# Sums of squares of the delta rule: an exact split into three bf16 numbers on GpSimd instead of one f32 product

## The reference

```python
def l2norm(x):
    xf = x.astype(jnp.float32)
    return (xf * lax.rsqrt(jnp.sum(xf * xf, axis=-1, keepdims=True) + 1e-6)).astype(x.dtype)
...
        q = l2norm(qkv[..., :GDN_KEY_DIM].reshape(bn, length, GDN_QK_HEADS, GDN_HEAD_DIM)) * (GDN_HEAD_DIM ** -0.5)
        k = l2norm(qkv[..., GDN_KEY_DIM:2 * GDN_KEY_DIM].reshape(bn, length, GDN_QK_HEADS, GDN_HEAD_DIM))
...
    def finish(o, z):
        bn_, _, length, _ = o.shape
        o = rmsnorm(o.transpose(0, 2, 1, 3), g_norm).reshape(bn_, length, GDN_VAL_DIM)
        return (o.astype(z.dtype) * jax.nn.silu(z)) @ w_out
```

## Time and profile before

| | |
|---|---|
| median of three runs | 3255.62 us |
| lowest and highest | 3249.88 and 5628.62 us |
| span of the profiled execution, first to last instruction | 3251.1 us |
| TensorE products busy | 3092.5 us, 95% |
| VectorE busy | 1731.2 us, 53% |
| ScalarE busy | 1539.1 us, 47% |
| GpSimd busy | 873.2 us, 27% |
| mean granted TensorE clock, share of full speed | 0.978 |

### The profile page before, as it was taken

One profiled execution on the slowest core, in us unless ns is written; L12 is line 12 of the kernel. 1 busy time (PEld: TensorE's weight loads), 2 busy tenths in 40 slices (PEclk: granted clock), 3 DMA queues, 4 the chain that ended last, 5 costly groups with the idle time before them and its releaser, 6 DMA issues. The chain is left out here.

```text
span 3251.1 us, 55663 instructions
## 1 busy us (share of the span) xinstructions
PE 3092.5 (95%) x21673; PEld 2016.4 (62%) x21673; DVE 1731.2 (53%) x3543; ACT 1539.1 (47%) x3296; POOL 873.2 (27%) x652
## 2 busy tenths in 40 slices
PE   5889999999999999999999999897999999999998
PEld 3357777777777764455445555444777777777753
DVE  1156666666666652244443334346676767776632
ACT  3155555555555531256432444335655565555521
POOL 0044434533533410011001101003544435343400
PEclk9699999999999999999999999898999999999999
DMA  9921111211211126022311111102212222121135
GB/s 375 330 68 54 56 56 55 67 56 45 72 56 51 45 89 235 1 68 64 128 33 31 29 46 52 72 4 80 66 53 69 59 60 63 57 68 53 43 120 192
DMA packets 224097, 261.93 MB, mean 81 GB/s; under 512 B 19418, under 2 KB 158948, under 8 KB 223716
## 3 DMA queue, kind: packets, MB, share of 16 engines
q1 hardware_dynamic: 223844, 258.46, 24.7%
HBM read 239.15 MB, written 19.27 MB: 79 GB/s over the span
## 5 line engine op out<-in xcount | busy, mean ns | idle before, releaser
L898 PE MATMUL ps<-hT,W 128*128 128x512 f32 (+1 forms) x2656 | 1001.2, 506 | 3.0 <-DVEq L192 2.0
L898 PEld LDWEIGHTS ps<-hT,W 128*128 128x128 f32 x2656 | 470.5, 193 | 195.1 <-issue 165.6
L1331 DVE CAST_PREDICATED arena<-mask,ps 128x384 bf16<-128x384 uint32 x448 | 253.2, 565 | 223.2 <-PE ps L967 174.3
L1148 ACT CAST arena<-ps 128x384 bf16<-128x384 f32 x384 | 166.9, 482 | 347.7 <-PE ps L954 346.7
L2372 PE MATMUL ps<-arena 128*128 128x512 f32 x712 | 311.2, 595 | 2.3 <-SPq L192 2.0
L1333 DVE CAST_PREDICATED arena<-mask,ps 128x384 bf16<-128x384 uint32 x448 | 250.9, 560 | 0.0
L2372 PEld LDWEIGHTS ps<-arena 128*128 128x128 f32 x712 | 134.5, 191 | 167.1 <-issue 162.8
L2007 PE MATMUL ps<-hT,W 128*128 128x512 f32 (+1 forms) x608 | 218.2, 493 | 0.6 <-DMA W<-in_att_w_in 0.4
L1455 POOL TENSOR_TENSOR arena<-arena 128x768 f32<-128x768 f32 (+1 forms) x32 | 44.4, 1389 | 636.0 <-ACT arena L1192 636.0
L1268 DVE SCALAR_TENSOR_TENSOR arena<-arena,vec 128x770 f32<-128x770 f32 (+1 forms) x192 | 205.4, 1070 | 6.8
L967 PEld LDWEIGHTS ps<-arena 128*128 128x128 bf16 x2304 | 144.7, 98 | 55.4 <-issue 51.0
(11 more groups left out here) (284 smaller groups left out, 6177.0 us busy)
## 6 DMA issues: line engine op xcount, KB each, us to landing
arena<-in_ada_w SPq DMA_DIRECT2D x24, 2048.0 KB, 19.5
W<-in_gdn_w_in SPq DMA_DIRECT2D x95, 512.0 KB, 4.0
arena<-decay_sums SPq DMA_DIRECT2D x64, 384.0 KB, 4.1
W<-decay_rows SPq DMA_DIRECT2D x64, 384.0 KB, 5.0
arena<-in_gdn_w_out SPq DMA_DIRECT2D x32, 512.0 KB, 10.5
W<-in_gdn_w_out SPq DMA_DIRECT2D x30, 512.0 KB, 3.4
arena<-gated SPq DMA_DIRECT2D x32, 384.0 KB, 7.7
gated<-arena SPq DMA_DIRECT2D x24, 384.0 KB, 2.3
```

The lines of the kernel that those rows point to most:

```text
L898: mm = pe.matmul(ps[:, b, 0:t1 - t0], w[:, i, :], env.hT[:, i, t0:t1], start=(i == 0), stop=(i == KD - 1))
L1148: act.copy(half_cols(Xb[d], s, d), ps[:, 2 * d, 0:384].rearrange("p (c b s) -> p c b s", c=NT, s=s)).then_inc(*inxe.up(m, lv, d))
L1331: dve.copy_predicated(half_cols(Mb[d], s, d), wide(env.m4[:, d, lv]), src_m).then_inc(*inm.up(m, lv, d, "m"))
```

## The change

One f32 square on GpSimd becomes five instructions: the square, its cast to bf16 (high part), the difference to it, the cast of the difference (middle part), and the difference to that, written as bf16 (low part). Each waits for the one before by a semaphore. The three parts add up to the f32 square. TensorE sums them by three bf16 products with a bf16 matrix of ones in one PSUM group, where one f32 product with f32 ones was. The matrix of ones is cast once per layer. The same holds for tiles (`squares`) and outputs.

```diff
-                    ("vtok", (NT, P)), ("ktok", (NT, P)), ("sz", (2, T)), ...
+                    ("vtok", (NT, P)), ("ktok", (NT, P)), ("sqhib", (T,)), ("sqmidb", (T,)), ("sqlowb", (T,)), ("onesb", (P,)), ("sz", (2, T)), ...
...
+    sqp = seq("x_parts", [(n, i) for n in TILES for i in range(4)])
+    osp = seq("o_parts", [(m, i) for m in U for i in range(4)])
...
-                mm = pe.matmul(ps[:, b, 0:t1 - t0], env.ones, v.sq[:, t0:t1], start=True, stop=True)
+                for part_at, exact in enumerate((v.sqhib, v.sqmidb, v.sqlowb)):
+                    mm = pe.matmul(ps[:, b, 0:t1 - t0], v.onesb, exact[:, t0:t1], start=(part_at == 0), stop=(part_at == 2))
...
+        def split(t, lo, parts, done, n):
+
+            whole, hi, mid, low = v.sq[:, lo:T], v.sqhib[:, lo:T], v.sqmidb[:, lo:T], v.sqlowb[:, lo:T]
+            pool.tensor_tensor(whole, t[:, lo:T], t[:, lo:T], ALU.mult).then_inc(*parts.up(n, 0))
+            pool.wait_ge(parts.sem, parts.at(n, 0))
+            pool.tensor_copy(hi, whole).then_inc(*parts.up(n, 1))
+            pool.wait_ge(parts.sem, parts.at(n, 1))
+            pool.tensor_tensor(whole, whole, hi, ALU.subtract).then_inc(*parts.up(n, 2))
+            pool.wait_ge(parts.sem, parts.at(n, 2))
+            pool.tensor_copy(mid, whole).then_inc(*parts.up(n, 3))
+            pool.wait_ge(parts.sem, parts.at(n, 3))
+            pool.tensor_tensor(low, whole, mid, ALU.subtract).then_inc(*done.up(n))
...
-            pool.tensor_tensor(v.sq[:, lo:T], t[:, lo:T], t[:, lo:T], ALU.mult).then_inc(*sqx.up(n))
-
+            split(t, lo, sqp, sqx, n)
+
+        pool.tensor_copy(v.onesb, env.ones)
...
-                ot = v.OT[:, n % 2, LO:T]
-                pool.tensor_tensor(v.sq[:, LO:T], ot, ot, ALU.mult).then_inc(*osq.up(n))
+                split(v.OT[:, n % 2], LO, osp, osq, n)
```

More of the change, by code:

```diff
@@ L635, in gdn_phase @@
     v = carve(env, [("pad", (2, PADW)), ("acc", (2, CONVW)), ("q", (T,)), ("k", (T,)), ("kS", (T,)), ("sq", (T,)),
-                    ("vtok", (NT, P)), ("ktok", (NT, P)), ("sz", (2, T)), ("KK", (NT, P)), ("QK", (NT, P)),
+                    ("vtok", (NT, P)), ("ktok", (NT, P)), ("sqhib", (T,)), ("sqmidb", (T,)), ("sqlowb", (T,)), ("onesb", (P,)), ("sz", (2, T)), ("KK", (NT, P)), ("QK", (NT, P)),
                     ("OT", (2, T)), ("S", (2, P)), ("R", (2, P)), ("V", (2, P)), ("VK", (2, P)), ("offneg", (P,)),
```

## The result

| | before | after |
|---|---|---|
| median of the runs | 3252.75 us (4 runs) | 3330.57 us (4 runs) |
| ratio, 95% interval | | 1.0251 [1.0228, 1.0275] |
| span of the profiled execution | 3251.1 us | 3333.8 us |
| TensorE products busy | 3092.5 us | 3102.0 us |
| mean granted clock | 0.978 | 0.971 |

A forecast was written before the change was run, and what follows sets the result against it. TensorE, busy throughout its slots, was taken as the bound. Losses of 65.6 us less a gain of 16.2 made net +49 us; 3251.1 + 49.4 + 4.5 = 3305 us, 1.5% slower, range 3258 to 3345.

The forecast's parts named there:

- TensorE's gain, 16.2: Sums in both delta layers: three bf16 products save 0.19 us per large sum, 0.10 per small, 16.2 us in all.
- rival 4: Sums: bf16 products of 512 columns stream at twice the packed rate, a large sum saves 0.52 us; 3284 us; 3%.
- Exposed waits, 21: Output sums in slots 14 and 15 of both layers: TensorE waits for the split, 21 us lost.
- The turns on the ports: Boundary after an even unit: VectorE and GpSimd alternate on shared SBUF ports; in layer 0 L1331 starts 3.6 us late.
- Rival 1: VectorE keeps the ports over back-to-back pairs, so only the exposed waits count: +5, 3260 us; 22%.
- Boundary in layer 0, 17.5: Seven boundaries after even units in layer 0: 2.5 us of TensorE stall each at L1012, 17.5 us.
- Odd slots in layer 0, 4.9: Last subtract delays L1354, VectorE is late to L1370, for which L1020 waits: 0.7 x 7 = 4.9 us.
- Layer 3, 7.7 + 9 + 2.5: Layer 3: boundaries after even units 7.7 us, its part of the work pushed later, query products meeting the second convolution 2.5.
- What is pushed later: GpSimd's low parts and caps move later and reach the convolution: 12 us in both layers, plus 2.5 for query products.
- After odd units, 0: Boundary after an odd unit: the two L1361 are delayed, but VectorE idles for longer than that, cost 0.
- Head sums, slot 16: 0: Head squares are ready in time; in the very last slot output-projection products stand ahead of the sum: cost 0.
- Rival 2: Every meeting of GpSimd and VectorE is paid in full, head squares of layer 3 late: +92, 3348 us; 21%.

The follow-up runs named there:

- pe_only: Kernel before with GpSimd's work unchanged, but TensorE sums three bf16 buffers of constants instead of the square: 3232.82 us, 0.9953 of before.
- tail_f32: Changed kernel, but the outputs of units 13 to 15 keep the f32 square and f32 product: 3304.50 us, 1.0181 of before.
- o_only: Changed kernel with the split for outputs alone; q and k tiles keep the f32 square and product: 3327.00 us, 1.0252 of before.
- x_only: Changed kernel with the split for q and k tiles alone; outputs keep the f32 square and product: 3245.70 us, 0.9992 of before.
- scores_caps: Changed kernel; the output's cast waits for the next unit's score products, and GpSimd's caps move between the identity matrices: 3275.76 us, 1.0094 of before.
- after_scores: Changed kernel with one wait added: the output's cast waits for VectorE's second score product of the next unit: 3357.31 us, 1.0347 of before.

## Why the prediction was near on the mechanism and low on the price

The sign and the walk at the boundary held. The chance that it would be over 2% slower was put at 30%, and that is what came. The forecast was a loss of 49 us, 82 came. (The 4.5 us that it adds for what lies around the span are 1.8 in the runs on record, 3335.6 for a span of 3333.8.) To weigh the terms of full slots I compare the slots of after with those of pe_only, which has TensorE's gain and none of GpSimd's work: 61.3 and 62.0 us in layer 0, after an even and after an odd unit, and 55.4 and 55.8 in layer 3.

- **TensorE's gain, 16.2:** near. 15 us in pe_only, 12 of them in its pairs of slots. In the trace of after, a small sum starts 0.33 us before its successor (751.62 to 751.95) where 0.43 was (732.72 to 733.15). Of a large sum the first record is missing; two records start 0.22 us apart each:

```profile
754.53 0.59 PE L907 MATMUL ps<-arena 128*128 128x512 bf16 x2
754.97 1.02 PE L900 MATMUL ps<-hT,W 128*128 128x512 f32 x2
```

  The f32 product ahead of it starts at 753.46 and takes 0.86 to its successor, so the sum has 754.32 to 754.97, 0.65 us where 0.86 was. It saves 0.21; the forecast had 0.19, rival 4 had 0.52 and is out.
- **Exposed waits, 21:** right in place, slightly low. 7.24 us at o0 of slot 14 in layer 0 where 0.70 was the earlier trace rows, 6.5 more for 6.2 forecast; 5.13 for 0.27 in layer 3, 4.9 for 4.3. The slots are 7.1 and 6.8 longer, since behind the wait TensorE runs at 0.50 of the clock for a while (the 0.80 us of three 256-column products is 0.49 elsewhere). tail_f32 gives back 23 to 26.
- **The turns on the ports:** right. The forecast's walk gave 10.01 us from L1412 to L1331; it is 10.02 or 10.03 at all seven boundaries of layer 0, for 6.38 before. In layer 3 it is 7.88 for 6.36, 1.5 more, and the forecast, 2.3 less 0.74 of idle time, had 1.6. Rival 1 (VectorE keeps the ports over a pair) is out.
- **Boundary in layer 0, 17.5:** the size of the stall right, its place wrong. It was priced as "TensorE's L1012 ... had 1.1 in hand: 2.5 us of stall". L1012 is not the first instruction that VectorE's lateness reaches. L945 waits 0.97 for ScalarE's cast of the late chunk matrix, and L1038, which needs the score products just ahead of the masks, waits 1.59, seven times; together that is 2.56, and that it meets the 2.5 from another path is luck. In the slots of o_only the boundary costs 3.1 us at full clock (64.8 for 62.0, and 0.3 gained), 22 us for seven.
- **Odd slots in layer 0, 4.9:** right in size, 4 us by the slots of x_only, with the wait at the masks and not at L1020.
- **A term that was missing: the clock.** This is the step that made most of the difference. Four of the seven slots of layer 0 are another 1.5 to 3.1 us longer (66.6 + 66.8 + 68.1 + 68.2, less 4 x 65.1 = 9.3 us) with the same idle time, and five of layer 3 are 1.6 us longer than the one of 57.4 at clock 1.00, 8 us: 17 us in the pairs, beside what stands behind the exposed waits. The forecast counted a stall as long as it lasts.
- **Layer 3, 7.7 + 9 + 2.5 (its part of the 12 is about 9), less 5 of gain: 14 forecast, 24.9 measured.** At full clock the slots after an even unit cost 13 us and those after an odd one 7, 20 us against the 19 of these terms; the clock's 8 and a gain of 3.6 for 5 are the difference. The mechanism "What is pushed later" is there: three L1271 of 512 take 5.20 us where 3.76 was the earlier trace rows, and TensorE then waits 1.26 and 0.58 us for the masks.

```profile
2520.88 5.20 DVE L1271 SCALAR_TENSOR_TENSOR arena<-arena,vec 128x512 f32<-128x512 f32 x3
```

```profile
2520.52 4.22 POOL L1441 TENSOR_TENSOR arena<-arena,cst 128x768 f32<-128x768 f32 x2
```

- **After odd units, 0:** not quite. A slot after an odd unit is 62.5 us in layer 0 and 57.1 in layer 3, 0.5 and 1.3 more than in pe_only, some 10 us in all. Whether the late score products or the later queue cost them was not tried; the forecast had them in part under "What is pushed later".
- **Head sums, slot 16: 0.** Right. GpSimd's wait appears only five times at the sums, four of them the exposed outputs; the fifth is 0.89 us at a head sum at the start of layer 3.

In the pairs of slots, then, the forecast's terms came to 45 us; 50 us are there at full clock, and 17 more by the clock. Rival 2, every meeting in full, was 3348, nearer in size than the forecast, but it had no clock in it: its 92 us of meetings less gain were worked out without the part of the loss that the clock made. Of TensorE's 73.2 us more of idle time the waits named above hold 17.2 (masks), 11.1 (scores), 23.7 (sums) and some 7 at L945, 59 in all; 6 more are at a product of another part that waits for its weights (L380). Of the last 8, some 5 are in front of the 512-column sums, in part only because their first records are missing. How the clock's loss divides between the stalls was not tried by itself; in scores_caps, where the stalls of the full slots are gone, it is gone there too.

## What to carry to other kernels

An engine at a third of its time is not free to take more work: ask which instructions of the others share its ports at that moment, and what stands behind them in their queue. When a queue is pushed later, follow every instruction in it to where it now lands, and price the first waiter of each late result, not the one that looks last; after_scores removed one meeting and lost more than that, 23 us on balance in the full slots, to the next. And look for work in such a queue that is due much later (here two caps): moving it was worth 11 us in the kernel before and 82 in after_scores. A repair that also helps the kernel before has to be measured against that kernel with the same repair.

## What the runs showed of the hardware

- **The granted clock can fall at stalls of 1 to 2 us inside a saturated stream, and does not every time.** After a stall of 1.58 us the clock was 0.50 and six products took 5.33 us; after one of 1.59 it was 1.00 and they took 2.74. In both cases a stall of 0.97 us stood some 3 us ahead.
- **Turns hold even for back-to-back instructions.** Two L1357 with no wait between them took 3.70 us beside GpSimd's split for 1.82 alone. The Trainium skill ("SBUF — State Buffer", section Who interferes with whom) says that who issues first holds the shared ports for its whole instruction; these rows agree, and add that the next turn goes to the other engine.
- **A VectorE instruction with one SBUF input can be held as well.** L1268 (L1265 before), a multiply by one scalar per partition, takes 0.61 us alone and 1.97 us beside GpSimd's L1496 (scores_caps, 338.29), a mean of 1.04 for 0.615. The same section of the Trainium skill names tensor_scalar among the operations that can take both port pairs; this trace agrees. The prediction named L1265 as reached by the later queue but gave these 24 us of VectorE's time no price of their own. In layer 0 they cost little: scores_caps keeps most of them (984 ns on average), and its slots are 62.0 us, no longer than before.
